# Head norms and rotation of a differential attention, moved from a stage of their own into the twelve blocks of the query, key and value weights

## The reference, cut to what matters

```
qkv = u @ w_qkv                                   # 512 x 1024 times 1024 x 3072
q = q.reshape(b, s, 8, 2, 64); k likewise; v = v.reshape(b, s, 8, 128)
q = rope(rms_norm(q, q_gain), cos, sin) * 64**-0.5
k = rope(rms_norm(k, k_gain), cos, sin)
# rms_norm: x * rsqrt(mean(x*x over the 64 of a head) + 1e-6) * gain
# rope:     (t1, t2) -> (t1*c - t2*s, t2*c + t1*s), t1 and t2 the two halves of the 64
scores = q @ k^T; p = softmax(scores); attn = p[:, :, 0] - lam * p[:, :, 1]; o = attn @ v
```

## Time and profile before

| what | value |
|---|---|
| profiled execution, span | 3332.79 us, 3331.1 us |
| PE busy | 2947.3 us, 88% |
| DVE busy, ACT busy | 1699.8 us (51%), 1125.6 us (34%) |
| chain that ended last: share of PE, DVE, ACT | 76%, 11%, 6% |
| DMA mean rate over the span | 94 GB/s |

### The profile page before, as it was taken

One profiled execution on the slowest core, in us unless ns is written; L12 is line 12 of the kernel. 1 busy time (PEld: TensorE's weight loads), 2 busy tenths in 40 slices (PEclk: granted clock), 3 DMA queues, 4 the chain that ended last, 5 costly groups with the idle time before them and its releaser, 6 DMA issues.

```text
span 3331.1 us, 39436 instructions
## 1 busy us (share of the span) xinstructions
PE 2947.3 (88%) x14938; PEld 2357.6 (71%) x14938; DVE 1699.8 (51%) x2474; ACT 1125.6 (34%) x1588; POOL 56.5 (2%) x42
## 2 busy tenths in 40 slices
PE   3999999998886789999999986879999884989998
PEld 2798678786674467778787782568788674778787
DVE  5566555655542556543333326847777554344242
ACT  2312233222323434433222328733233342443231
POOL 1003000000000000000000000000000000000000
PEclk7999899999996889799999997999999996999999
DMA  5550444555433000023332320014344554223232
GB/s 180 164 152 1 121 114 133 157 141 142 141 114 116 1 1 1 1 63 93 103 89 85 104 91 0 1 51 101 116 152 145 171 177 86 52 77 100 90 98 66
DMA packets 447010, 315.83 MB, mean 95 GB/s; under 512 B 13490, under 2 KB 435484, under 8 KB 446876
## 3 DMA queue, kind: packets, MB, share of 16 engines
q1 hardware_dynamic: 327056, 232.80, 23.9%
q10 hardware_dynamic: 119820, 81.18, 8.3%
HBM read 292.00 MB, written 19.86 MB: 94 GB/s over the span
## 4 chain that ended last, share of the span: by engine, by line
PE 76%; DVE 11%; ACT 6%; issue 4%; DMA 2%; ACTq 1%; POOL 1%; DVEq 0%; POOLq 0%
PE ps L435 52%; PE ps L417 4%; PE ps L429 3%; PE ps L836 2%; DMA ada_ring<-in_ada_w 1%; PE ps L2440 1%; DVE ada_ring L1615 1%; PE ps L822 1%; PE ps L809 1%; ACT L608 1%; PE ps L1524 1%; DVE ada_ring L486 1%; PE ps L1489 1%; DVE ada_first L500 1%; DVE h_area L1619 1%
## 5 line engine op out<-in xcount | busy, mean ns | idle before, releaser
L435 PE MATMUL ps<-hh,whi 128*128 128x512 f32 x1744 | 691.2, 396 | 5.1 <-DVE xT L2274 2.7
L435 PE MATMUL ps<-hh,wlo 128*128 128x512 f32 x1744 | 682.6, 391 | 0.0
L435 PE MATMUL ps<-hl,whi 128*128 128x512 f32 x1744 | 682.5, 391 | 0.0
L389 DVE TENSOR_TENSOR wlo<-raw,whi 128x2048 fp32r<-128x2048 f32 x198 | 453.8, 2292 | 404.7 <-ACT whi L385 404.7
L385 ACT ACTIVATE whi<-raw 128x2048 fp32r<-128x2048 f32 x198 | 377.2, 1905 | 421.6 <-PE ps L435 257.6
L435 PEld LDWEIGHTS ps<-hh,whi 128*128 128x128 f32 x1744 | 329.9, 189 | 78.4 <-issue 10.0
L435 PEld LDWEIGHTS ps<-hl,whi 128*128 128x128 f32 x1744 | 329.9, 189 | 69.8 <-issue 2.4
L435 PEld LDWEIGHTS ps<-hh,wlo 128*128 128x128 f32 x1744 | 329.6, 189 | 69.7
L435 PE MATMUL ps<-hid_h,whi 128*128 128x512 f32 x756 | 309.5, 409 | 0.2
L435 PE MATMUL ps<-hid_l,whi 128*128 128x512 f32 x756 | 300.3, 397 | 0.0
L435 PE MATMUL ps<-hid_h,wlo 128*128 128x512 f32 x756 | 300.0, 397 | 0.0
(11 more groups left out here) (379 smaller groups left out, 4434.7 us busy)
## 6 DMA issues: line engine op xcount, KB each, us to landing
raw<-in_ffn_w_in SPq DMA_DIRECT2D x44, 1024.0 KB, 6.0
ada_ring<-in_ada_w ACTq DMA_DIRECT2D x80, 512.0 KB, 4.1
raw<-in_ffn_w_up SPq DMA_DIRECT2D x32, 1024.0 KB, 5.4
raw<-in_ffn_w_down SPq DMA_DIRECT2D x32, 1024.0 KB, 6.1
raw<-in_ffn_w_out SPq DMA_DIRECT2D x32, 704.0 KB, 4.7
raw<-in_hgrn_w_in SPq DMA_DIRECT2D x16, 1024.0 KB, 5.5
raw<-in_attn_w_qkv SPq DMA_DIRECT2D x12, 1024.0 KB, 5.2
s_area<-cp_dram SPq DMA_DIRECT2D x6, 2048.0 KB, 10.3
```

Of the source, the lines that this page charges most:

```text
L389: nc.vector.tensor_tensor(wlo[:, par, :], raw[:, par, :], whi[:, par, :].bitcast(F32), ALU.subtract).then_inc(w_lo, 1)
L435: m = nc.tensor.matmul(ps[:, bank, :], tile(w, kt, j), x[:, kt, :], start=(kt == 0 and n == 0), stop=(kt == k - 1 and n == 2))
```

## The change

The stage of head norms goes away. Its work is hung into the bodies of the twelve blocks:

- **Evacuation** (`gained`): ACT takes each result of q and k out of PSUM twice, once multiplied by the gain and once squared. The squares lie in four buffers (`sq` and `xn` together). Before its first one ACT waits until all of `hl` is written (and `xn` free), and for the small values of DVE.
- **Sums**: after blocks 1 to 8 PE sums the squares of two tiles (the pair of results of the block before), 16 matmuls in all, into PSUM banks 4 to 7.
- **Functions over four tiles**: ACT does one Ln over 128 x 2048 after blocks 2, 4, 6, 8 and one Exp over 128 x 2048 after blocks 3, 5, 7, 9.
- **Swap by transfers** (`d_turn`): the rotation by matmul goes. SP issues four DMAs for each pair of tiles, from block 4 on, each behind the load of a block: they copy 32 partitions by 1024 elements (128 KB) from the pair to `d_rot`, with the 32-row halves of each head swapped. The sign goes into the sine table once, at the start (`diff_dve_start`).
- **Rotation** (`d_hook_dve`, blocks 1 to 8): DVE waits for the transfers of the pair of the block before, then does three operations over 128 x 1024; from block 4 on it also multiplies the pair of four blocks before by its root (the factor is the same for both halves of a head, so it may come after the rotation). Both stand ahead of `convert_lo` in DVE's list.
- The three segments are unrolled on all engines.

```diff
         HN0, RP0 = len(qk_items), 16
+        dn_sum, dn_log, dn_rs, dn_rot, dn_rdy = hn_ss, hn_sq, hn_rs, rp_ps, rp_rdy
+        D0 = {"d_q": 0, "d_k": 4, "d_v": 8}
+        d_rot = nsa_area[:, 17664:21760].rearrange("p (k t) -> p k t", k=8)
+        d_rs = nsa_area[:, 13568:17664].rearrange("p (k t) -> p k t", k=8)
+        turned_in = ((g_in, CMP_LOADS), (nsa_in, 80))
+
+        def d_square(u):
+            return (sq, xn)[u % 4 // 2][:, u % 2, :]
+
+        def d_pair(db):
+            return (dq, dk)[db // 4][:, 2 * (db % 4):2 * (db % 4) + 2, :]
+
+        def d_turn(sp, db):
+
+            sp.wait_ge(ev_a, seg["d_q"].ea0 + 2 * db + 2)
+            if db >= 4:
+                sp.wait_ge(dn_rot, RP0 + 2 * db - 6)
+            slots = slice(2 * db % 8, 2 * db % 8 + 2)
+            for row in range(0, P, 32):
+                sp.dma_start(d_rot[row:row + 32, slots, :], d_pair(db)[row ^ 32:(row ^ 32) + 32, :, :]
+                             ).then_inc(turned_in[db % 2][0], 16)
+
...
+            if 1 <= db <= 8:
+                for u in (2 * db - 2, 2 * db - 1):
+                    pe.wait_ge(ev_a, seg["d_q"].ea0 + u + 1)
+                    if u >= 4:
+                        pe.wait_ge(dn_log, HN0 + u - 3)
+                    nc.tensor.matmul(ps[:, 4 + u % 4, :], blk64, d_square(u), start=True, stop=True
+                                     ).then_inc(dn_sum, 1)
...
+            if db >= 2 and db % 2 == 0 and db <= 8:
+                u = 2 * db - 4
+                act.wait_ge(dn_sum, HN0 + u + 4)
+                if u >= 8:
+                    act.wait_ge(dn_rdy, RP0 + u - 4)
+                nc.scalar.activation(d_rs[:, u % 8:u % 8 + 4, :], ps[:, 4:8, :], ACT.Ln, scale=1.0 / 64,
+                                     bias=eps_col[:, :]).then_inc(dn_log, 4)
+            if db >= 3 and db % 2 and db <= 9:
+                u = 2 * db - 6
+                act.wait_ge(dn_log, HN0 + u + 4)
+                r = d_rs[:, u % 8:u % 8 + 4, :]
+                nc.scalar.activation(r, r, ACT.Exp, scale=-0.5).then_inc(dn_rs, 4)
...
+            if 1 <= db <= 8:
+                b = db - 1
+                ready, base = turned_in[b % 2]
+                x, r = d_pair(b), d_rot[:, 2 * b % 8:2 * b % 8 + 2, :]
+                wide = lambda c: c.unsqueeze(1).broadcast_to((P, 2, T))
+                dve.wait_ge(ready, base + 64 * (b // 2 + 1))
+                tt(r, r, wide(sinT), ALU.mult)
+                link(tt(x, x, wide(cosT), ALU.mult))
+                tt(x, x, r, ALU.add).then_inc(dn_rot, 2)
+            if db >= 4:
+                b = db - 4
+                u = 2 * b
+                dve.wait_ge(dn_rs, HN0 + u + 2)
+                dve.wait_ge(dn_rot, RP0 + u + 2)
+                x = d_pair(b)
+                tt(x, x, d_rs[:, u % 8:u % 8 + 2, :], ALU.mult).then_inc(dn_rdy, 2)
...
         def diff_pe(pe):
-            pe.wait_ge(nsa_in, 80)
             boundary(pe, seg["d_out"])
-            r = head_norm_pe(pe, HN0, 2 * KT, dif_turns, RP0)
-            pe.wait_ge(rp_rdy, r)
+            pe.wait_ge(dn_rdy, RP0 + 2 * KT)
...
         def diff_act(act, link):
-            act.wait_ge(lam_sum, 1)
-            nc.scalar.activation(d_small[:, 2:4], d_small[:, 4:6], ACT.Exp).then_inc(lam_exp, 1)
-            act.wait_ge(ev_v, after(seg["d_v"])[2])
-            head_norm_act(act, link, HN0, dif_items)
...
+            link(nc.vector.tensor_reduce(d_small[:, 7:8], rotm, AX.X, ALU.add))
+            link(nc.vector.tensor_scalar(sinT, sinT, d_small[:, 7:8], -1.0, ALU.mult, ALU.mult))
...
+                elif s.name in D0:
+                    for b in range(s.n):
+                        load(b, (s.g0 + b) % 2, True)
+                        if D0[s.name] + b >= 4:
+                            d_turn(sp, D0[s.name] + b - 4)
...
-                linear(seg["d_q"], to_tile(seg["d_q"], [(ACT.Copy, dq, 1.0)]))
-                linear(seg["d_k"], to_tile(seg["d_k"], [(ACT.Copy, dk, 1.0)]))
+                act.wait_ge(hl_rdy, 6 * KT)
+                act.wait_ge(lam_sum, 2)
...
+                def gained(s, dst, gain):
+                    def evac(b, par):
+                        for j in range(2):
+                            u = 2 * (D0[s.name] + b) + j
+                            act.wait_ge(mm, s.mm0 + 2 * b + j + 1)
+                            if u >= 4:
+                                act.wait_ge(dn_sum, HN0 + u - 3)
+                            x = ps[:, 2 * par + j, :]
+                            nc.scalar.activation(dst[:, 2 * b + j, :], x, ACT.Copy, scale=gain)
+                            nc.scalar.activation(d_square(u), x, ACT.Square).then_inc(ev_a, 1)
+                    return evac
+                linear(seg["d_q"], gained(seg["d_q"], dq, d_small[:, 0:1]))
+                linear(seg["d_k"], gained(seg["d_k"], dk, cols_b[:, GR + 5:GR + 6]))
...
                     evac(b, par)
+                    if s.name in D0:
+                        d_hook_dve(dve, link, D0[s.name] + b)
                     if more:
                         convert_lo(dve, s, b, par, 2)
```

More of the change, by code:

```diff
@@ L368, in each_block, with unrolled @@
                 body(b, (s.g0 + b) % 2, s.g0 + b + 2 < blocks)
-        def unrolled(s, body, hook):
+        def unrolled(s, body, first, hook):
             for b in range(s.n):
                 body(b, (s.g0 + b) % 2, s.g0 + b + 2 < blocks)
-                hook(G0[s.name] + b)
+                hook(first[s.name] + b)
         def landed(s, b, par, ahead):
@@ new lines, in d_hook_pe, with d_hook_act @@
+        def d_hook_pe(pe, db):
+            if db == 1:
+                pe.wait_ge(nsa_in, 80)
+            if 1 <= db <= 8:
[5 more added lines that the diff above has]
+                                     ).then_inc(dn_sum, 1)
+        def d_hook_act(act, db):
+            if db >= 2 and db % 2 == 0 and db <= 8:
[10 more added lines that the diff above has]
+                nc.scalar.activation(r, r, ACT.Exp, scale=-0.5).then_inc(dn_rs, 4)
+            if db == 3:
+                act.wait_ge(lam_sum, 1)
+                nc.scalar.activation(d_small[:, 2:4], d_small[:, 4:6], ACT.Exp).then_inc(lam_exp, 1)
@@ new lines, in d_hook_dve @@
+        def d_hook_dve(dve, link, db):
+            tt = nc.vector.tensor_tensor
+            if 1 <= db <= 8:
[14 more added lines that the diff above has]
+                tt(x, x, d_rs[:, u % 8:u % 8 + 2, :], ALU.mult).then_inc(dn_rdy, 2)
@@ L1120, in diff_pool, with diff_dve_start @@
                 nc.gpsimd.tensor_tensor(d_sq, do[:, t, :], do[:, t, :], ALU.mult).then_inc(df_sq, 1)
-        def diff_dve(dve, link):
+        def diff_dve_start(dve, link):
+            link(nc.vector.tensor_scalar(d_small[:, 0:1], cols_b[:, GR + 4:GR + 5], 0.125, None, ALU.mult))
+            s = ROWS["attn_subln_2"]
             dve.wait_ge(nsa_in, 80)
@@ L1128, in diff_dve @@
             nc.vector.tensor_reduce(d_small[:, 4:6], pr, AX.X, ALU.add).then_inc(lam_sum, 1)
-            s = ROWS["attn_subln_2"]
             nc.vector.tensor_scalar(d_small[:, 1:2], cols_b[:, s:s + 1], 1.0 - LAM_INIT, None, ALU.mult
                                     ).then_inc(lam_sum, 1)
-            link(nc.vector.tensor_scalar(d_small[:, 0:1], cols_b[:, GR + 4:GR + 5], 0.125, None, ALU.mult))
+            link(nc.vector.tensor_reduce(d_small[:, 7:8], rotm, AX.X, ALU.add))
+            link(nc.vector.tensor_scalar(sinT, sinT, d_small[:, 7:8], -1.0, ALU.mult, ALU.mult))
+        def diff_dve(dve, link):
             dve.wait_ge(lam_exp, 1)
@@ L1135, in diff_dve @@
                                                 in1=d_small[:, 2:3], op0=ALU.add, op1=ALU.subtract))
-            dve.wait_ge(ev_a, after(seg["d_k"])[1])
-            head_norm_dve(dve, link, HN0, dif_items, dif_ropes, RP0)
             def combine(v):
@@ L2056, in linear @@
                 if s.name in G0:
-                    unrolled(s, body, lambda gb: prep_act(act, gb))
+                    unrolled(s, body, G0, lambda gb: prep_act(act, gb))
+                elif s.name in D0:
+                    unrolled(s, body, D0, lambda db: d_hook_act(act, db))
                 else:
@@ L2254, in linear @@
                 if s.name in G0:
-                    unrolled(s, body, lambda gb: prep_dve(dve, link, gb))
+                    unrolled(s, body, G0, lambda gb: prep_dve(dve, link, gb))
+                elif s.name in D0:
+                    unrolled(s, body, D0, lambda db: None)
                 else:
@@ L2356, in _ @@
                 apply(5, 4, cols_b[:, r:r + 8], None, after(seg["ffn1_out1"])[0])
+                diff_dve_start(dve, link)
                 linear(seg["d_q"], none)
@@ L2475, in linear @@
                 if s.name in G0:
-                    unrolled(s, body, lambda gb: prep_pe(pe, gb))
+                    unrolled(s, body, G0, lambda gb: prep_pe(pe, gb))
+                elif s.name in D0:
+                    unrolled(s, body, D0, lambda db: d_hook_pe(pe, db))
                 else:
```

## The result

Four runs of the changed kernel took 3276.87 to 3287.76 us, median 3283.39. The kernel before took 3334.61 in the same series (four runs). The ratio is 0.9846, 95% interval 0.982 to 0.9873. The forecast of 3278 against its base of 3332.8 is 0.9836. The profiled execution is the one of 3276.87 us, with a span of 3275.0.

A forecast was written before the change was run, and what follows sets the result against it. PE was taken to bound the projections, with the head-norm stage also on the path. 3332.8 - 79.5 (stage) + 13.8 (sums) - 1.1 (k/v wait) + 11.5 (ring) = 3277.5, say 3278 us; range 3264 to 3297.

The forecast's parts named there:

- Part 1, the stage of head norms goes: Between block 11's last product and the attention's first maximum: 84.2 us shrink to 4.7, -79.5 us.
- Part 2, the sums: On PE after blocks 1 to 8: two full float32 matmuls of 512 columns each time, 8 x 1.72 = +13.8 us.
- The wait between k and v: PE's wait there for ACT's last evacuation (1939.20 to 1940.27) is filled by the sums: -1.1 us.
- Part 3, ACT and the rest: In the blocks: ACT's worst body needs 7.8 of 12.6 us, DVE's start work fits idle time; 0 us.
- the possible 3.5 us of slower blocks: Blocks beside new work might run at 11.20 instead of 10.88 us, up to 3.5 us; taken as 0.
- The other small term: PE reaches the attention at full clock, perhaps gaining 1 or 2 us in its first scores; taken as 0.
- Part 4, the ring: In DVE's bodies: conversion, load, swaps, rotation, next conversion wait on each other; PE stalls from block 6 on, +11.5 us.
- L: Time from the load's issue to the fourth swap's landing: 5.2 + 2.6 = 7.8 us, forecast band 7.2 to 8.6.
- The swaps are hidden: Rival at the rotation's transfers: L of 6.6 or less, stall 0 to 2, 3266 to 3268 us; chance 0.25.
- The swaps are slower: Rival at the rotation's transfers: L from 8.9 to 10.5, stall 20 to 33, 3286 to 3299 us; chance 0.23.
- In series: Rival at each body's first rotation: each swap awaits the previous landing, 3334 or 3375 us; chance 0.04.
- ACT as the bound: Rival in the blocks: ACT replaces PE as bound, needing over 12.6 us per body; late ACT shares chance 0.05.

The follow-up runs named there:

- the two versions without the ring: Changed kernel with DVE's rotation moved behind the conversion: 3263.39 us, ratio 0.9798; changed kernel with SP's swaps issued ahead of the load: 3263.35 us, ratio 0.979.

## Why the prediction was right, point by point

**The mechanisms were right; the term of the ring was too small, and the total came close partly by luck.** The stage came to 172.1 us. By the forecast's terms it is 221.6 - 79.5 + 13.8 - 1.1 + 11.5 = 166.3.

- *Part 1, the stage of head norms goes* (84.2 to 4.7). The last product of block 11 ends at 2011.94, the first maximum starts at 2016.36: 4.4 us. Right.
- *Part 2, the sums* (+13.8). 1.72 us between two blocks, shown by doubling as well. Right. Their price is that of full float32: in rounded form two cost 0.46. The wait between k and v is gone; that the sums covered it was shown by the version with short sums, in which 0.80 us of it came back. Without the ring the terms give 221.6 - 79.5 + 13.8 - 1.1 = 154.8 us, and the two versions without the ring measured 154.3.
- *Part 3, ACT and the rest* (0). Ln 1.97 and Exp 1.91 us over 128 x 2048, as worked out. ACT has more room than was claimed: where no ring binds, table loads twice as often cost nothing. The blocks beside the new work ran at 10.90, so the possible 3.5 us of slower blocks did not come. The other small term, 1 or 2 us from a better clock in the first scores, stays undecided: the granted clock there was 0.94 (2016.4 to 2026 us) against 0.67 before (2070.8 to 2080), and the span behind the stage fell by 1.7 us, but among all the versions it differs by up to 5.6.
- *Part 4, the ring* (+11.5). The mechanism is right in each of its signs: DVE waits eight times for DMA at the rotation, PE waits for the conversion from block 6 on. The size was too small: it was 17.8. **The term that was mis-sized is L, 8.77 us instead of 7.8.** The forecast set the transfers one behind the other, 5.2 for the load and 2.6 for the swaps. They mix: the load lands after 6.6 us in the median, and the last swap after it.

How the 0.97 comes about is shown only in part. In the group of 1956.08 us, with L at 8.61, data flow for 6.5 us; apart, the load's flow took some 3.7 and that of the swaps some 2.5, in the version with the swaps ahead. So by these views mixing makes the flow longer by about 0.3 us. Another 0.5 lies behind the last data, 1.0 us until the rotation where the load alone took 0.5 to land. And one body of 9.82 raises the mean by 0.15; why its load landed so late is open.

The arithmetic of the miss: 8 x 0.97 = 7.8 us more from L. DVE's part of the ring was shorter, 5.92 instead of 6.19 us in bodies 1 to 3 and 7.06 instead of 7.44 in bodies 4 to 8, in all some 2.6: two of its operations in a row can overlap by 0.09 us (operations of 1.22 us start 1.14 us apart), and the 0.2 allowed in each body for handovers was 0.02. The ring also started 0.6 us sooner, 19.8 us after the start of the stage instead of 20.4. DVE ended its eighth body at +143.0 us from the start of the stage and not at +138.4, so 4.6 of the miss came this way. The remaining 1.2 lies behind it: the last two blocks took 24.56 us instead of 2 x 11.58, 1.4 more, and the end of the stage 0.3 less than forecast. There the clock shows. Windows of the changed kernel, right behind PE's last wait of 3.84 us, and the stretch after it:

```profile
1987.38:1991.50 4.12, 4.12 (x24) 4.12 (x25) 4.12 (x4) 1.39 (x1) 0.00 (x0) 0.65 0.71 219
1991.50:1995.00 3.50, 3.50 (x32) 3.50 (x31) 0.67 (x2) 0.00 (x0) 0.00 (x0) 1.00 0.65 194
```

For some 3 us the matmuls start 0.21 us apart, at the 1.2 GHz level (granted clock 0.65 over the first stretch), and then 0.12 apart at 2.4 GHz. Blocks 6 and 8, each behind a wait, are longer in the same way (12.83 instead of 11.47 us, 13.16 instead of 11.96 without the ring), but there the ring sets when the next block can start, and the loss disappears in the next wait. These stretches are some 4.1 of PE's 5.8 us of longer busy time. Most of the rest is at the restarts: block 7, behind a wait of 0.76 us and with no slow stretch, took 12.94 us with its sums instead of 12.62.

That the total of the profiled execution, 3276.9, agrees with 3278 is luck: 6.6 us of difference in code that did not change hid the 5.8 us by which the stage was too long. The median of the runs is 5.4 us above the forecast, and by the ratio (0.9846 measured, 0.9836 forecast) it is between 3 and 4 us too low, the direction of the miss in L.

**The rivals.** *The swaps are hidden* fell with the first wait at L1081; it needed L of 6.6. *The swaps are slower* came near. L of 8.77 lies above the forecast's own band, which ends at 8.6, and just below that rival's, which begins at 8.9; the stall of 17.8 lies at the upper edge of the forecast's 7 to 18. By the forecast's own formula, 8 x (L - 6.35), an L of 8.77 would have meant 19.4. What spoke for that rival, that these DMAs touch few partitions, is also what the copy over 128 partitions points to. *In series* fell with L: it needed 14.7 by the formula (the forecast wrote 14.6). *ACT as the bound* fell with the version that works over two tiles, where 10.3 us more of table loads changed nothing.

On the Trainium skill, "SBUF — State Buffer": its section "Door 1: The DMA port swizzle" says that a transfer over 32 partitions reaches half of the ports. The runs here point its way, since 512 KB in one DMA over 128 partitions made L 1.5 us shorter than in four over 32, though the number of issues changed with it. The summary of the same page of the Trainium skill reckons with 436 GB/s for transfers within SBUF. The four DMAs over 32 partitions stayed far below, at about 205 GB/s alone and 219 to 260 in a backlog; the one over 128 partitions, mixed with the end of the load, came to 416 to 448.

**What stays open.** Form and number of issues were changed together in the copy over 128 partitions, so that the form makes the difference is likely and not proven. A swap in fewer DMAs that still reverses the halves was not tried. Why the load in one body of the ring lands 2 us later than in the others isn't known.

## What to carry to other kernels

A wait that is hung into a list ahead of recurring work closes a ring if its releaser is issued behind that work's result. Then a microsecond of the transfer costs as many microseconds as there are bodies, and saving work on the busiest engine brings next to nothing (8.6 us became 0.9). Put the consumer of a slow transfer behind the recurring work, or its issue ahead, and either takes the ring apart. When two transfers share a queue, don't add the landing of the one to the flow of the other: read from the trace how both land together, and reckon with the first one becoming later too.

## What the runs showed of the hardware that was not expected

- A load of 1 MB that lands in 5.2 us alone took 6.5 to 6.7 us in the median when four DMAs of 128 KB were issued behind it in the same queue. With one DMA of 512 KB behind it, it took 5.9.
- A backlog of DMAs of 128 KB within SBUF, 32 partitions each, flowed at 219 to 260 GB/s with the DMA engines nine tenths busy. One of 512 KB over 128 partitions, with the end of a load, flowed at 416 to 448.
- Waits of PE of 2.6 to 4.1 us were followed by stretches of about 3 us at the lower clock level (the blocks behind them 1.2 to 1.5 us longer). In one case the stretch began at once, in another 1.5 us after the restart (block 6); behind waits of 0.6 and 0.8 us there was none.
- Two DVE operations in a row over 128 x 1024 start 1.14 us apart though each is shown as 1.22. Where the second needs the result of the first (L1083 behind L1082) it is 1.32.
